# From expert 10 to 29, half of the weight loads issued from ScalarE's queue instead of SyncE's

## What is computed

```python
def expert_block(args):
    rows, ex = args
    xb = x_ext[rows]
    gu = xb @ w1[ex] + b1[ex]
    gate = jnp.minimum(gu[:, :D_FF_EXPERT], SWIGLU_LIMIT)
    up = jnp.clip(gu[:, D_FF_EXPERT:], -SWIGLU_LIMIT, SWIGLU_LIMIT)
    glu = gate * jax.nn.sigmoid(gate * SWIGLU_ALPHA)
    return ((up + 1.0) * glu) @ w2[ex] + b2[ex]
```

## Time and profile before

| what | value |
|---|---|
| timed runs | 1121.81, 1122.79 and 1125.68 us, median 1122.79 |
| span of the profiled execution (first to last instruction) | 1120.1 us |
| mean granted TensorE clock | 0.998 |
| PE / DVE / ACT busy, share of the span | 95% / 27% / 10% |
| read from HBM | 434.66 MB, 389 GB/s over the span |

### The profile page before, as it was taken

The page is one execution under the profiler, slowest core; times in us unless marked ns, Lnnn a source line. Parts: engine busy times, 40 slices in busy tenths (PEclk is TensorE's granted clock), DMA queues, the critical chain, the costliest instruction groups (busy, mean ns, idle before and its releaser), DMA issues.

```text
span 1120.1 us, 13354 instructions
## 1 busy us (share of the span) xinstructions
PE 1066.7 (95%) x5293; PEld 475.6 (42%) x5293; DVE 303.6 (27%) x656; ACT 114.1 (10%) x243; POOL 43.2 (4%) x44
## 2 busy tenths in 40 slices
PE   8999999999999999999999999999999999999997
PEld 7888888633333333333333333333333333333332
DVE  4356644322222222222222222222121112222213
ACT  1042520200000000000000000000000000000001
POOL 1106500000000000000000000000000000000000
PEclk9999999999999999999999999999999999999999
DMA  9953369599999999999999999999999999999996
GB/s 358 419 214 128 113 260 383 204 374 429 428 427 428 429 429 426 429 430 429 425 429 430 429 427 427 431 429 429 425 430 430 429 425 428 431 429 429 425 425 270
DMA packets 35783, 436.05 MB, mean 389 GB/s; under 512 B 4432, under 2 KB 4944, under 8 KB 6992
## 3 DMA queue, kind: packets, MB, share of 16 engines
q1 hardware_dynamic: 34752, 434.77, 92.7%
q10 hardware_dynamic: 1008, 0.95, 0.3%
HBM read 434.66 MB, written 1.05 MB: 389 GB/s over the span
## 4 chain that ended last, share of the span: by engine, by line
PE 74%; DMA 17%; SPq 5%; DVE 3%; ACT 1%; issue 1%; another core or an unknown queue 0%; POOL 0%; POOLq 0%; DVEq 0%
PE bank L862 29%; DMA ring<-in_w 16%; PE bank L924 16%; PE bank L595 5%; SPq L364 5%; PE bank L836 4%; PE bank L786 4%; PE bank L792 3%; PE bank L696 2%; PE bank L678 2%; PE bank L539 2%; DVE work L1333 2%; PE bank L591 1%; PE bank L764 1%; PE bank L517 1%; PE bank L643 1%
## 5 line engine op out<-in xcount | busy, mean ns | idle before, releaser
L862 PE MATMUL bank<-ring,work 128*64 128x512 f32 x2048 | 450.9, 593 | 19.3 <-DMA ring<-in_w 18.7
L862 PEld LDWEIGHTS bank<-ring,work 128*64 128x64 f32 x2048 | 147.7, 137 | 301.9 <-issue 273.2
L924 PE MATMUL bank<-ring,work 128*64 128x512 f32 x1024 | 234.1, 599 | 18.0 <-DVE work L1333 17.5
L924 PEld LDWEIGHTS bank<-ring,work 128*64 128x64 f32 x1024 | 67.8, 136 | 141.4 <-issue 114.9
L1323 DVE TENSOR_SCALAR work<-bank 128x512 f32<-128x512 f32 x32 | 22.1, 692 | 388.2 <-PE bank L862 388.2
L1505 ACT ACTIVATE work<-work 128x512 f32<-128x512 f32 x32 | 20.2, 630 | 723.0 <-DVE work L1323 723.0
L836 PE MATMUL bank<-work 64*128 64x512 f32 x256 | 63.6, 615 | 0.9 <-DVE work L1303 0.9
L786 PE MATMUL bank<-x2n,work 128*64 128x512 f32 x256 | 61.9, 604 | 0.8 <-DVE work L1238 0.8
L1249 DVE TENSOR_TENSOR work<-bank,vec 128x256 f32<-128x256 f32 x64 | 24.2, 420 | 134.5 <-PE bank L792 134.5
L792 PEld LDWEIGHTS bank<-cst,work 128*128 128x128 f32 x320 | 33.8, 140 | 54.2 <-issue 49.5
L595 PE MATMUL bank<-ring 128*128 128x256 f32 x240 | 54.2, 382 | 0.0
(11 more groups left out here) (194 smaller groups left out, 572.4 us busy)
## 6 DMA issues: line engine op xcount, KB each, us to landing
ring<-in_w SPq DMA_DIRECT2D x184, 2048.0 KB, 40.7
ring<-in_w_in SPq DMA_DIRECT2D x16, 1024.0 KB, 23.8
ring<-in_w SPq DMA_DIRECT2D x15, 1024.0 KB, 12.8
ring<-in_w_out SPq DMA_DIRECT2D x4, 1024.0 KB, 4.9
ring<-in_w_up_a SPq DMA_DIRECT2D x2, 1024.0 KB, 9.5
ring<-in_w_up_b SPq DMA_DIRECT2D x2, 1024.0 KB, 6.2
ring<-in_na_rpb SPq DMA_DIRECT2D x1, 1536.0 KB, 17.6
ring<-in_w SPq DMA_DIRECT2D x2, 512.0 KB, 29.3
```

The lines of the kernel that those rows point to most:

```text
L862: last = pe.matmul(bank[CAP * a:CAP * (a + 1), bk, :], kT, pairs[:, pair_of(par, k // 2), at + q * 512:at + (q + 1) * 512], start=False, s ...
L924: last = pe.matmul(bank[CAP * a:CAP * (a + 1), to, :], fT, pairs[:, pair_of(par, c), at + a * 512:at + (a + 1) * 512], start=f == 0, stop= ...
```

## The change

From expert 10 to expert 29, SP issues blocks 0, 2 and 4, and ACT issues blocks 1, 3 and 5, on its own queue. Slots, semaphores, sizes, and the condition on `chunk_used` stay as they were. Experts 0 to 9 and the last two, 30 and 31, are loaded by SP alone as before. On ACT the issues stand between the blocks of its own work: after its part of expert b come block 5 of expert b + 1, then blocks 1 and 3 of expert b + 2, each behind its own wait on `chunk_used`.

```diff
+        SHARED = 10
+        SP_BLOCKS, ACT_W1, ACT_W2 = (0, 2, 4), (1, 3), 5
...
-            with sp.Fori(2, E // 2 - 1) as j:
+            with sp.Fori(2, SHARED // 2) as j:
                 for par in range(2):
                     for c in range(BLK):
+                        load_chunk(2 * j + par, c, par, (2 * j + par - 2) * BLK + (PRE + c + 1))
+            with sp.Fori(SHARED // 2, E // 2 - 1) as j:
+                for par in range(2):
+                    for c in SP_BLOCKS:
                         load_chunk(2 * j + par, c, par, (2 * j + par - 2) * BLK + (PRE + c + 1))
...
+            def load_pair(e, c, par):
+
+                act.wait_ge(chunk_used, (e - 2) * BLK + (PRE + c + 1))
+                act.dma_start(pairs[:, pair_of(par, c), :], pair_source(e, c)).then_inc(pair_landed[par][c], 16)
+
+            def load_w1(e, par):
+
+                for c in ACT_W1:
+                    load_pair(e, c, par)
+
             expert_block(0)
-            with act.Fori(1, E - 1) as b:
+            with act.Fori(1, SHARED - 2) as b:
                 expert_block(b)
+            expert_block(SHARED - 2)
+            load_w1(SHARED, 0)
+            with act.Fori(SHARED // 2, E // 2 - 1) as j:
+                expert_block(2 * j - 1)
+                load_pair(2 * j, ACT_W2, 0)
+                load_w1(2 * j + 1, 1)
+                expert_block(2 * j)
+                load_pair(2 * j + 1, ACT_W2, 1)
+                with act.If(j < E // 2 - 2):
+                    load_w1(2 * j + 2, 0)
+                act.nop()
+            expert_block(E - 3)
+            expert_block(E - 2)
             expert_block(E - 1, last_one=True)
```

More of the change, by code:

```diff
@@ L340, in projected, with pair_source @@
             return half_(BF)[:, 1, :] if (c, a) == (0, 1) else half_(c % 3)[:, a, :]
+        def pair_source(e, c, cols=slice(0, PAIR_F)):
+            w, at = (w1, c) if c < W1_CH else (w2, c - W1_CH)
+            return w[bass.ds(e, 1), :, at, cols].rearrange("e p n -> p (e n)")
         block = ctx.enter_context(nc.Block())
@@ L364, in load_chunk @@
                 sp.dma_start(pairs[:, pair_of(par, c), :], pair_source(blk, c)).then_inc(pair_landed[par][c], 16)
-            def pair_source(e, c, cols=slice(0, PAIR_F)):
-                w, at = (w1, c) if c < W1_CH else (w2, c - W1_CH)
-                return w[bass.ds(e, 1), :, at, cols].rearrange("e p n -> p (e n)")
             def load_half(blk, c, par, part, landed):
```

## The result

The change makes the kernel a little slower. Its median is 1127.12 us (8 runs, 1126.01 to 1128.41) against 1123.15 us for the kernel before (8 runs, 1121.81 to 1126.28): a ratio of 1.0036, with a 95% interval of 1.0027 to 1.0045. That is 4.0 us, just past the 3.4 us (0.3%) that can be told from no change, with the interval on both sides of that bound. The profiled execution took 1126.06 us, 2.3 us more than its span of 1123.8 us; the span before was 1120.1, so 3.7 us are to be found.

What follows compares the result with a forecast made beforehand. DMA was taken to bound the kernel, never resting from 252 us on, with 19.1 us behind its last landing in the chain. 1120.1 + 0 + 0 + 0 of span plus 2.7 gave 1122.8 us, range 1116 to 1132.

Steps and rivals of the forecast that it cites:

- a late block at the end of the stretch: Rival at experts 28 and 29: block 5 of 29 lands late and DMA rests; 9.8 us, 1132.6 us, chance 0.04.
- Moved loads, no change of rate: The 60 loads moved to ACT's queue keep their rate, 587.6 us at 428.3 GB/s; bounds 7.6 us less, 4.6 more.
- changing queues costs at each packet: Rival, 455 to about 1050 us: engines pay at each queue switch; 0.8 to 1.5% more, 1127 to 1132, chance 0.14.
- DMA does not rest: In the shared stretch ACT's later issues leave at least 4.7 blocks in flight, so DMA never rests; cost 0.
- ACT's own work: Three issues of 0.47 us ahead of ACT's next sigmoid, covered by 22.05 us idle; uncovered, 1.4 us an expert.
- ACT held: Rival at ACT's issues: held up to 11.4 us each, 12.1 us an expert, up to 240 us; chance 0.03.
- Added code: ACT's and SP's loops grow; one or two more code fetches are 0 to 2.2 us, taken as 0.
- Is a block late for PE?: Shared experts: block 5, called tightest, has 31.5 us and three blocks take 29.4, so it fits barely; cost 0.
- a miss only moves a wait of PE's forward: PE's weight waits: DMA works on while PE waits for an issued block, so a late block costs 0.
- Marks: Signs written beforehand of a right or wrong forecast: queue bytes, rate, late period, ACT's issues, landings and idle time.
- more than about 19 us behind the last landing: Sign of a wrong forecast: more work behind the chain's last DMA landing than the 19.1 us of before.

Runs made afterwards that it cites:

- e3: The changed kernel with only experts 28 and 29 shared, SP alone loading 4 to 27: 1130.69 us, ratio 1.0069 to the kernel before.
- e5: The changed kernel with sharing begun at expert 4 and ended at 27, SP alone loading 28 and 29: 1131.99 us, ratio 1.0081 to the kernel before.
- e6: The changed kernel with blocks swapped, ACT issuing 0, 2 and 4 and SP 1, 3 and 5: 1129.61 us, ratio 1.0061 to the kernel before.
- e1: The changed kernel with only experts 10 to 27 shared, SP alone loading 28 and 29: 1123.61 us, ratio 1.0003 to the kernel before.
- e2: The changed kernel with only experts 10 to 28 shared, SP alone loading 29: 1124.46 us, ratio 1.0015 to the kernel before.
- e7_again_a: The changed kernel itself run once more, nothing altered: 1126.27 us, span 1124.1, beside 1123.51 us for the kernel before.

## Why the prediction was right and wrong

The forecast was 1122.8 us with a range of 1116 to 1132; the range holds 1127.12. That is in part luck, since its upper end stood for a cost of changing queues and for DMA at rest, and neither came. And the likeliest case, no difference within 0.3%, did not come: +0.36% is a small loss, and the case that it belongs to, a late block at the end of the stretch, had a chance of 0.04. Step by step:

- **Moved loads, no change of rate: right.** 428 GB/s against 429 over 500 us, and packet for packet in turn, as the earlier trace rows had it. The last landing moved by 0.4 us. The forecast had this from the start of the program, with small rows, and it held for 16 KB rows. Of the rival "changing queues costs at each packet" nothing is left (e3).
- **DMA does not rest: right.** From the tenth slice to the last but one none is under 423 GB/s. The reckoning by blocks in flight is also borne out from its other side: e5, which begins where less is in flight, does let DMA rest.
- **ACT's own work and ACT held: right.** 1.58 us for three issues, under a cover of 25 us; the longest issue took 0.445 us. The rule of the Trainium skill, page "Perfetto Trace Analysis", section "DMA Instruction — HWDGE (DVE, Sync)", by which one issuing engine could be held by the other, shows no cost in this trace. SP's own long issues are gone as well while both queues run, with fewer blocks in each (0.33 to 0.34 us, where they took up to 11.4).
- **Added code: right.** 17 packets of code on queue q8 in both profiles, and 7 where there were 6 on q14, 0.01 MB.
- **"Is a block late for PE?": this step failed,** twice. First, it named block 5 as the tightest and reckoned with it alone. For block 5 the reckoning was good: three blocks in ACT's queue, 29.4 us, against a measured 30.6, and 31.5 to be had. But block 3 was never reckoned. By the same means: it is issued third, some 1.2 us behind block 5, so 19.95 us into an expert, and read two experts later after three quarters of the outer product, 54.3 + 10.3 = 64.6, which leaves 44.7 us. Ahead of it in ACT's queue stand not two blocks but four, the two issued with it and blocks 1 and 3 of the expert before; five turns of 9.79 are up to 49.0 us. Measured: 47.3. It does not fit, by 2.6 us.
- Second, the step said that **"a miss only moves a wait of PE's forward"**, and priced it at nothing. Inside the stretch that is so: PE's first wait for weights came at 691.9 us, where it was 746.0 before, two experts sooner, and its waits in all are 0.8 us shorter. At the end of the stretch it is not, since there are no experts left in which PE would have waited anyway. The right question was not whether DMA stays busy, but which block lands at the hand-over, and what work lies behind it.
- **The rival "a late block at the end of the stretch" had the place right and the mechanism wrong.** It let DMA rest for want of free slots and priced that at two blocks, 9.8 us. DMA did not rest. The price is one block's time less the slack of the end, 4.7 - 1.0 = 3.7 us. Against it I had set that SP's loads for expert 30 keep DMA busy; they do, and it does not help.
- **Marks.** q10, rate, period, ACT's issues and idle time came as written (landings from 13.7 us on, where I had said 20). The mark for being wrong that did appear is "more than about 19 us behind the last landing" of the chain: 79.4 us.

The sum mended by that term: 1120.1 + 3.7 = 1123.8 of span.

## What to carry to other kernels

Splitting one stream of loads over two hardware queues leaves the rate as it is where one queue already fills it, but it changes the order: a single queue delivers in order of need, two that take turns deliver in pairs, and a block was late here by one block's time for each block needed after it that came with it or ahead of it (one in the change, two in e6). While DMA sets the pace this can't be seen; it is paid where the pace passes back to the compute engine. So end such a split early enough for the compute engine to win the delay back (here two experts, e1; with one, e2, some of it stayed). Begin it while that engine still lives on a stock (e3 began too late), but not before enough loads are in flight to keep DMA busy (e5 began too early). When a wait is said to cost nothing because it "only moves", look for the last place to which it can move.

## What the runs showed of the hardware that I had not expected

**A wait of 2 us can take TensorE's clock with it.** PE's timeline of after, block 3 of three experts in a row, and the window around the second (columns as in the earlier trace rows; the clock is the last but two):

```profile
721.28 3.65 PE L868 MATMUL bank<-ring,work 128*64 128x512 f32 x16 [2.00 <-DMA ring<-in_w]
...
750.64 5.35 PE L868 MATMUL bank<-ring,work 128*64 128x512 f32 x16 [1.99 <-DMA ring<-in_w]
...
780.04 3.65 PE L868 MATMUL bank<-ring,work 128*64 128x512 f32 x16 [0.33 <-DMA ring<-in_w]
```

```profile
745.00:774.00 29.00, 26.45 (x120) 8.83 (x118) 5.98 (x13) 1.61 (x3) 0.00 (x0) 0.94 1.01 431
```

Four times in the change, at 750.6, 838.8, 926.9 and 985.7 us, the granted clock falls to the lower of its two levels (1.2 of 2.4 GHz) for part of a block that follows such a wait, and its 16 matmuls take 5.35 us and not 3.65. In the kernel before, with the same waiting cut into pieces of 0.6 and 1.15 us, the granted clock of that window is 1.00 and there is no such fall while the weights stream. Not each wait of 2 us is followed by one (721.28 is not). Here the 1.7 us are nearly always free, since the next wait is shorter by as much (0.33 us at 780.04); the mean clock of 0.992 against 0.998 looks like a cause of the loss and is none. e1 tells the two apart: it has four such falls as well, at a mean clock of 0.993, and no loss. Only the last one, behind which PE never waits again, is paid in e1 (1.7 us of its 1120.9). The change run again, e7_again_a, has five falls and the span of the change to 0.3 us: its last, at 1015.29, only leaves a wait of 0.32 us in place of 2.00 ahead of the block at 1044.68.

**A newly begun queue goes ahead of a long one.** With some ten blocks in SP's queue, ACT's first ones land past them (e3), and the block that PE needs is 6.04 us late. The Trainium skill, page "DMA: Bandwidth & Descriptors", section "Issuing engines are not separate DMA queues", says that issuing from several engines saves only the sequencer's time. The rate here agrees (428 GB/s by two queues, 429 by one); the order of the landings, and with it 3.7 us here and 8.7 us of span in e3, is what comes on top.
